# Recurrent stage of a two-block model: order of row loads, key blocks, the first preparation and two clearing steps

## The reference, cut to what matters

```python
mod = cond @ ada_w[l] + ada_b[l]            # shift, scale, gate of a layer, 3072 values
h = rms_norm(x, norm_g[l]) * (1.0 + scale) + shift
z = h @ even_w_in[j]
a_val, a_glu, a_gate, r, k, v, wd, ad, b_gate = split_cols(z, EVEN_SIZES)
ya = conformer_conv(a_val, a_glu, conv_w[j], conv_vec[j]) * silu(a_gate)
...
r, k, v, wd, ad = (lerp(t, mu) for t in (r, k, v, wd, ad))   # z + (shifted z - z) * mu
w_log = -softplus(-(w0 + tanh(wd) @ w_up)) - 0.5
decay = exp(-exp(w_log));  a = sigmoid(a0 + ad @ a_up)
kk = heads(k * k_k);  kk = kk / max(sqrt(sum(kk * kk)), 1e-12)
k = k * (1.0 + (a - 1.0) * k_a)
# scan over 512 tokens, for each of 16 heads of 64:
sa = state @ (-kk);  state = state * w + sa (kk * a)^T + v k^T;  y = state @ r
bonus = sum(r * k * r_k) * v
```

## Time and profile before

| | us |
|---|---|
| median of 3 runs | 3185.33 |
| lowest and highest | 3184.12, 3186.64 |
| the profiled execution | 3184.31 |
| its span in the trace | 3182.5 |
| busy PE in it | 3065.3 (96%) |

### The profile page before, as it was taken

How to read it: one execution, slowest core, us unless ns; L and a number is a source line. 1 busy time by engine, 2 the same in 40 slices (tenths; PEclk the granted TensorE clock), 3 DMA queues, 4 the chain that set the end, 5 groups by cost and what they waited for, 6 DMA issues and landing times.

```text
span 3182.5 us, 38153 instructions
## 1 busy us (share of the span) xinstructions
PE 3065.3 (96%) x15318; PEld 2415.8 (76%) x15318; DVE 2131.8 (67%) x3453; ACT 1236.4 (39%) x1768; POOL 862.2 (27%) x550
## 2 busy tenths in 40 slices
PE   8799999999999999999999999999999999999997
PEld 4467877677677666877887788878888888888886
DVE  3678888758789766574889899456665444444445
ACT  3234444335333655424333566533223222233224
POOL 2243443222344110143455422322222110111100
PEclk9899999999999999999999999999999999999998
DMA  7121111335222111332244467766554334333341
GB/s 258 60 96 53 51 50 58 112 101 173 75 86 73 40 40 35 107 104 90 83 139 133 138 217 231 241 220 198 185 193 152 108 124 126 119 126 119 113 132 53
DMA packets 167568, 382.91 MB, mean 120 GB/s; under 512 B 10848, under 2 KB 77408, under 8 KB 167264
## 3 DMA queue, kind: packets, MB, share of 16 engines
q1 hardware_dynamic: 167392, 380.48, 37.1%
HBM read 320.14 MB, written 60.29 MB: 120 GB/s over the span
## 4 chain that ended last, share of the span: by engine, by line
PE 75%; DVE 15%; ACT 5%; POOL 2%; DMA 2%; issue 1%; SPq 0%; DVEq 0%; ACTq 0%; POOLq 0%
PE ps L747 20%; PE ps L749 20%; PE ps L748 20%; DVE oh L2416 2%; PE ps L1148 2%; DVE at L2154 2%; PE ps L1076 2%; DVE ai L2152 1%; PE ps L915 1%; PE ps L1056 1%; PE ps L935 1%; POOL wsp L2517 1%; PE ps L889 1%; POOL pk L2633 1%; DVE at L2142 1%
## 5 line engine op out<-in xcount | busy, mean ns | idle before, releaser
L747 PE MATMUL ps<-hT,wsp 128*128 128x512 f32 x2016 | 825.7, 410 | 35.8 <-POOL wsp L2517 16.2
L2517 POOL TENSOR_TENSOR wsp<-ring,wsp 128x1024 fp32r<-128x1024 f32 x207 | 512.8, 2480 | 1061.4 <-ACT wsp L1203 1016.7
L749 PE MATMUL ps<-hT,wsp 128*128 128x512 f32 x2016 | 790.8, 392 | 0.0
L748 PE MATMUL ps<-hT,wsp 128*128 128x512 f32 x2016 | 789.5, 392 | 0.0
L747 PEld LDWEIGHTS ps<-hT,wsp 128*128 128x128 f32 x2016 | 381.0, 189 | 142.9 <-issue 24.2
L749 PEld LDWEIGHTS ps<-hT,wsp 128*128 128x128 f32 x2016 | 380.4, 189 | 82.9
L748 PEld LDWEIGHTS ps<-hT,wsp 128*128 128x128 f32 x2016 | 381.6, 189 | 80.5 <-issue 9.1
L2640 POOL TENSOR_TENSOR ex<-ex 128x512 fp32r<-128x512 f32 x128 | 176.0, 1390 | 831.4 <-ACT ex L1600 831.4
L1203 ACT ACTIVATE wsp<-ring 128x1024 fp32r<-128x1024 f32 x311 | 321.8, 1051 | 99.0 <-PE ps L749 80.7
L2440 DVE TENSOR_TENSOR xT<-ps,xT 128x512 f32<-128x512 f32 x256 | 174.7, 688 | 259.8 <-PE ps L749 259.8
L747 PE MATMUL ps<-ex 128*128 128x512 f32 x808 | 314.9, 390 | 2.0 <-DVE ex L1660 2.0
(11 more groups left out here) (406 smaller groups left out, 4784.1 us busy)
## 6 DMA issues: line engine op xcount, KB each, us to landing
ring<-in_eu SPq DMA_DIRECT2D x128, 512.0 KB, 3.6
ring<-in_ev SPq DMA_DIRECT2D x128, 512.0 KB, 3.6
gd<-oh SPq DMA_DIRECT2D x8, 4096.0 KB, 15.0
ex<-gd SPq DMA_DIRECT2D x32, 1024.0 KB, 6.7
ring<-in_ein SPq DMA_DIRECT2D x57, 512.0 KB, 3.7
ring<-in_oin SPq DMA_DIRECT2D x39, 512.0 KB, 3.5
ex<-zd SPq DMA_DIRECT2D x17, 1024.0 KB, 9.3
ring<-in_ada SPq DMA_DIRECT2D x30, 512.0 KB, 3.7
```

Of the source, the lines that this page charges most:

```text
L747: pe.matmul(out, W[0], R[0], start=first, stop=False)
L748: pe.matmul(out, W[0], R[1], start=False, stop=False)
L749: return pe.matmul(out, W[1], R[0], start=False, stop=last)
L2517: pool.tensor_tensor(s[:, 1, :], raw_of(i), s[:, 0, :].bitcast(F32), ALU.subtract).then_inc(pool_done, G.step("lo", i))
```

## The change

Four edits, all in the recurrent stage.

1. **Row loads.** `number` numbers the units in the order of their first use. The four row loads of a group are now put singly before the four quarters of one dense block (`among`): in iteration 1 three groups among the blocks of r, v and `val`, in iteration 7 three among r, v and the gate block, in iteration 8 one among the second gate block. Before, they followed each other with only what `PLACES` put between.
2. **Key first.** The blocks of a pair come as k, r, v in place of r, k, v. The parities of `z_copy` stay as they are.
3. **First preparation.** The blocks k, r and v of pair 0 join the lane of the first preparation, and `PLACES["first"]` spreads its pieces from place 190 to 900 of the whole; before, all but the last stood in the stretch of `val` and `glu` of two blocks behind k, r and v.
4. **Clearing.** `blank` is done for one matrix set at a time: set 0 before `mu`, set 1 at place 900 of the first preparation. The byte mask is a piece of its own (`mask`), behind the v block.

```diff
-    "first": (283, 303, 346, 351, 359, 425, 425, 513, 523, 523, 523, 523, 523, 523, 810, 863, 872, 882),
+    "first": (190, 235, 275, 316, 340, 360, 380, 434, 480, 560, 580, 600, 620, 640, 710, 730, 760, 790, 900),
...
     def number(pieces):
-        loads = []
-        for x in pieces:
-            if x[0] == "ada" or x[0] == "dense" and x[3] == 0:
-                rows = 0
-                while x[0] == "dense" and rows < min(2, len(loads)) and loads[-1 - rows][0] == "ada":
-                    rows += 1
-                loads.insert(len(loads) - rows, x)
-        at = {x: unit("ada" if x[0] == "ada" else "ein", x[4]) for x in loads}
         for x in pieces:
             if x[0] == "ada":
-                order.append((*x[:4], at[x]))
+                order.append((*x[:4], unit("ada", x[4])))
             elif x[0] == "dense":
                 if x[3] == 0:
-                    open_[x[1], x[2]] = at[x]
+                    open_[x[1], x[2]] = unit("ein", x[4])
...
     def rkv(c):
-        return [*dense("r", c, 24 + c), *dense("k", c, 32 + c), *dense("v", c, 40 + c)]
+        return [*dense("k", c, 32 + c), *dense("r", c, 24 + c), *dense("v", c, 40 + c)]
...
+    def among(row, block):
+
+        return [x for pair in zip(row, block) for x in pair]
...
+    order.append(("blank", 0))
     number(dense("mu", 0, 48))
-    number(rkv(0))
-    order.append(("blank",))
-    lane = [*conv_in(0), *conv_in(1)]
-    number([x for _, x in sorted(spread(lane) + placed(prep(0), "first"), key=lambda y: y[0])])
-    mods = {7: [1, 2, 3], 8: [4]}
+    lane = [*dense("k", 0, 32), *dense("r", 0, 24), *dense("v", 0, 40), ("mask",), *conv_in(0), *conv_in(1)]
+    number([x for _, x in sorted(spread(lane) + placed([*prep(0), ("blank", 1)], "first"), key=lambda y: y[0])])
     for i in range(1, 10):
+        rows = {1: [(0, 4), (0, 5), (1, 0)], 7: [(1, 1), (1, 2), (1, 3)], 8: [(1, 4)]}.get(i, [])
...
-        lane = turned_late(lane)
+        lane = turned_late([x for b in range(0, len(lane), 4) for x in (
+            among(ada(*rows[b // 4 - 1]), lane[b:b + 4]) if 0 < b // 4 <= len(rows) else lane[b:b + 4])])
...
-            def blank():
-                for z in abk:
-                    dve.memset(z, 0.0).then_inc(vector_done, V.step())
+            def blank(z):
+                dve.memset(abk[z], 0.0).then_inc(vector_done, V.step())
+                own()
+                for e in range(2):
...
+            def mask():
                 w.wait_ge(tensor_done, T("pp", 7))
                 w.wait_ge(pp_out, 128)
                 w.wait_ge(rw_in, 96)
                 dve.tensor_copy(msk, msum.bitcast(U32)).then_inc(vector_done, V.step("msk"))
...
             def ab(c, d, cc):
-                w.wait_ge(vector_done, V("blank"))
+                w.wait_ge(vector_done, V("blank", c % 2))
+                w.wait_ge(vector_done, V("msk"))
```

More of the change, by code:

```diff
@@ L160, in number @@
     def number(pieces):
-        loads = []
-        for x in pieces:
-            if x[0] == "ada" or x[0] == "dense" and x[3] == 0:
-                rows = 0
-                while x[0] == "dense" and rows < min(2, len(loads)) and loads[-1 - rows][0] == "ada":
-                    rows += 1
-                loads.insert(len(loads) - rows, x)
-        at = {x: unit("ada" if x[0] == "ada" else "ein", x[4]) for x in loads}
+        n = None
         for x in pieces:
             if x[0] == "ada":
-                order.append((*x[:4], at[x]))
+                order.append((*x[:4], unit("ada", x[4])))
             elif x[0] == "dense":
                 if x[3] == 0:
-                    open_[x[1], x[2]] = at[x]
+                    open_[x[1], x[2]] = unit("ein", x[4])
                 order.append((*x[:4], open_[x[1], x[2]]))
@@ L220, in schedule @@
     order.append(("rw_begin",))
+    order.append(("blank", 0))
     number(dense("mu", 0, 48))
-    number(rkv(0))
-    order.append(("blank",))
-    lane = [*conv_in(0), *conv_in(1)]
-    number([x for _, x in sorted(spread(lane) + placed(prep(0), "first"), key=lambda y: y[0])])
-    mods = {7: [1, 2, 3], 8: [4]}
+    lane = [*dense("k", 0, 32), *dense("r", 0, 24), *dense("v", 0, 40), ("mask",), *conv_in(0), *conv_in(1)]
+    number([x for _, x in sorted(spread(lane) + placed([*prep(0), ("blank", 1)], "first"), key=lambda y: y[0])])
     for i in range(1, 10):
+        rows = {1: [(0, 4), (0, 5), (1, 0)], 7: [(1, 1), (1, 2), (1, 3)], 8: [(1, 4)]}.get(i, [])
         lane = [*(rkv(i) if i <= 7 else gates(range(STORED)) if i == 8 else []),
-                *(x for g in mods.get(i, ()) for x in ada(1, g)),
                 *(dense("bgate", i - 2, 47 + i) if 2 <= i < 9 else []), *(conv_in(i + 1) if i <= 6 else [])]
-        if i == 1:
-            lane = [*dense("r", 1, 25), *ada(0, 4), *dense("k", 1, 33), *ada(0, 5), *dense("v", 1, 41), *ada(1, 0), *conv_in(2)]
         if i == 9:
@@ L1791, in rw_begin @@
                 V.here("zero")
-            def blank():
-                for z in abk:
-                    dve.memset(z, 0.0).then_inc(vector_done, V.step())
+            def blank(z):
+                dve.memset(abk[z], 0.0).then_inc(vector_done, V.step())
+                own()
+                for e in range(2):
+                    dve.tensor_copy(mats[z][0][:, e, :, 0, :], ident[:, :].rearrange("p (o n) -> p o n", o=1).broadcast_to(
+                        [128, CH, 128])).then_inc(vector_done, V.step("blank", z))
+            def mask():
                 w.wait_ge(tensor_done, T("pp", 7))
@@ L1799, in blank @@
                 dve.tensor_copy(msk, msum.bitcast(U32)).then_inc(vector_done, V.step("msk"))
[L1800 to L1804, removed]
             def dense_part(kind, i, p, n):
@@ L2491, in vector_program @@
             walk({"ada": ada, "turned": turned, "turned5": turned5, "square": square, "stat": stat, "freed": freed, "raw": raw,
-                  "norm": norm, "norm_nf": norm_nf, "rw_begin": rw_begin, "blank": blank, "dense": dense_part, "tap": tap,
+                  "norm": norm, "norm_nf": norm_nf, "rw_begin": rw_begin, "blank": blank, "mask": mask, "dense": dense_part, "tap": tap,
                   "knr": knr, "mix": mix, "decay": decay, "inv": inv, "hats": hats, "bonus": bonus, "ab": ab, "p1": p1,
```

## The result

| | us |
|---|---|
| before, median of 20 runs | 3184.34 (3178.57 to 3190.19) |
| after, median of 20 runs | 3189.99 (3182.70 to 3195.40) |
| ratio after / before | 1.0018, interval 1.0011 to 1.0025 |
| profiled execution of after, its span | 3188.88, 3187.1 |

The forecast was 3169.3, faster, in a range of 3160 to 3181; the kernel is slower by some 6 us, about the 0.2% that can be told from no change. By the profile's page PE is busy for as large a share as before, and for 5.5 us longer.

A forecast was written before the change was run, and what follows sets the result against it. PE, busy for 96% of the span, bounds the kernel; only its waits and lower clock can be recovered. Gains 2 + 12 + 0 + 2 = 16 us off 3184.3 give 3168.3, plus 1.0 for the median: 3169.3, range 3160 to 3181.

The forecast's parts named there:

- First preparation: Stretch before iteration 1: first `ab` at about 115.0 in place of 117.05, gain 2 us, bounds 7 and a loss of 2.
- The chain: First preparation: scans end at 90.9, `hats` at 98.0, so `bonus` waits about 9.4 us and `turn` 0 another 0.9.
- The clock behind the wait: First preparation, PE work behind the wait at `bonus`: half clock costs about 1.8 us, as behind the 7.35 us.
- Iteration 1: Recurrent stage, iteration 1: 77.9 us in place of 89.79, a gain of 12 us, bounds 15.5 and 6.
- signs of error: Wrong if a low-half wait were 4 us, iteration 1's clock stayed 0.92, or `bonus` came before 94 or after 102 us.
- ideal work: Iteration 1 without PE's idle time and clock loss: 89.8 - 15.2 - 6 = 68.6 us.
- The term of 2 us for the pairs pulled apart: Iteration 1: back-to-back row loads cost less than two apart, so splitting the pairs was taken to cost 2 us.
- Iterations 7 and 8: Recurrent stage, iterations 7 and 8: gain 6.7 + 2.2 - 5.5 - 1.4 = 2 us, bounds -3 and +6.
- the 6.7 us of waits that I struck out: Iterations 7 and 8: all PE idle time, 128.60 - 121.95 = 6.7 us, counted as gain.
- The new halves eat more: Rival: waits of v 1, val 2, v 7 and gate block each bring about 3 us half-clock loss; 3179, chance 0.15.
- Slower: Rival: high halves start only after PE's preceding piece, hiding nothing at five blocks; 3195.6 us, chance 0.06.
- The fill of set 0: Rival: the fill delays POOL's low half of k, PE loses 3.3 us at first k block; 3172.6, chance 0.04.

The follow-up runs named there:

- late_bonus: Changed kernel with `bonus` and the three `turn` moved among the last `glu` block's quarters, second clearing at place 30: 3190.68 us, 1.0022 of before.
- prep_late: Changed kernel with decay, `inv` and `hats` behind `glu` 0, `bonus` and `turn` at 955 to 995, second clearing at 30: 3177.88 us, 0.9976 of before.
- turned_on: Changed kernel with dense units numbered up to two row loads earlier and each `turned` one piece of the lane later: 3174.91 us, 0.9974 of before.
- pulled: Changed kernel with before's `number`: dense units behind row loads loaded and split up to two row loads earlier: 3181.27 us, 0.9989 of before.
- best_a: turned_on with row loads in a row in iterations 7 and 8 and the places of late_bonus: 3172.19 us, 0.9966 of before.
- best_b: turned_on with the places of prep_late and row loads in a row in iteration 7 alone: 3164.91 us, 0.9935 of before.

## Why the prediction was wrong, step by step

**First preparation (forecast a gain of 2, measured 0.1 to 1.7).** The chain was right: `bonus` at 97.56 for 98, a wait of 9.55 for 9.4, `turn` at 0.78 for 0.9, scans at 6.61 for 5 or more. The rule of the Trainium skill, "SBUF — State Buffer", section "Who interferes with whom", that a VectorE instruction with two SBUF inputs contends with a GpSimd instruction that reads SBUF, is borne out once more by 6.61 against 1.45 us. The clock behind the wait was mis-sized: 1.8 us were taken from the wait of 7.35 us, but PE worked at the lower level from 97.6 to about 106.8 (clock 0.51 there), which is some 4 us of loss. In eight profiles the preparation took 64.5 us on the mean, against 65.7 in two of the old order: a gain of about 1. And one move had no price at all: the product of `glu` 0 now stood behind the whole preparation, with val 1 behind it on PE. late_bonus shows that wait, and prep_late against late_bonus that this place was worth 9.4 us.

**Iteration 1 (forecast 77.9, measured 90.7).** The load waits went, `ab` waited 1.91 us for 1.9 forecast, and none stood at v 1 (1.6 forecast). The terms that failed: val 2, 5.47 for 1.7, since I followed ACT's order to the low half and not POOL's, where `mix` stood ahead and waited for DVE; `turned` before `lora`, 1.59 for 0.6; the rest 3.7 for 1.5. Sum of waits 12.7 for 7.3. With 68.6 + 2 of work that makes 83.3, and the remaining 7.4 us are the clock, 0.91 of full, where I had taken the loss of 6 us as gone. Both, a wait of over 4 us on a low half and this clock, were named ahead as signs of error. With the low halves early and `turned` moved the same sum nearly closes: 68.6 + 2 + 8.5 = 79.1, clock 0.98, measured 80.3. So the forecast's ideal work was right to some 2 us; its waits and its clock were not those of this order. The term of 2 us for the pairs pulled apart isn't borne out: from start to next start the twelve row loads took 13.4 us after and 12.8 before, and only one pair of them stood back to back in the trace of before.

**Iterations 2 to 6**: 0, as forecast.

**Iterations 7 and 8 (forecast a gain of 2, measured a loss of 7.6).** Single row loads: from start to next start, the 16 of them took 15.55 us for 14.18 before, 1.4 as forecast. The gate block: 2.38 for 2.4. What failed: of the 6.7 us of waits that I struck out, 1.7 were waits of the inversion (0.78 us and less) that no edit touched, and 2.1 of such waits, with two of the solution, stand in the new trace; v 7 took 2.74 for 1.0, because ACT's square root with its table load stood ahead of the high half; the waits at `turned` and behind it came to 3.2 for 2.1; and the clock, where 2.2 us were to come back, lost 2 more. These are 2.1 + 1.7 + 1.1 + 4 = 8.9 of the 9.6 us missed; the rest isn't assigned.

**Rivals.** "The new halves eat more" named the mechanism, but priced it at 3179 with 0.15: it counted no other term as mis-sized. "Slower" (3195.6) needed 3.6 us exposed at five blocks; the trace has 5.5, 2.7 and 2.4 at three of them and none at v 1 and `glu` 2. The fill of set 0 held nobody up: 3.47 us, beside two low halves of 2.38 us each, the fill as in the kernel before, the halves as on the mean (DVE, then POOL):

```profile
54.33 3.47 DVE L1788 MEMSET rw<- 128x4096 f32 x1 [0.80 <-issue]
57.84 2.87 DVE L1791 COPY rw<-ident 128x512 f32<-128x512 f32 x2
```

```profile
54.48 4.76 POOL L2512 TENSOR_TENSOR wsp<-ring,wsp 128x1024 fp32r<-128x1024 f32 x2 [7.19 <-ACT wsp L1197]
```

**What stays open.** The profiled stages leave after 7.6 us behind before at 730 us, the profiled executions differ by 4.6 and the medians by 5.7: some 2 to 3 us come back in the rest of the kernel, whose order is the same, unexplained. And by what the clock falls: see below.

## What to carry to other kernels

When an edit takes away a wait for a transfer by spreading the transfers, ask at once when each engine *between* transfer and use gets to its step: here ACT's high half and POOL's low half stood in fixed orders behind steps that wait for DVE, and moved with them. A wait is only removed if the next thing in the queue has its bank, its halves and its shared tile; so follow the bank's reader through that engine's own order (prep_late's 12 us) before moving the piece that waits. And strike out only those waits that you can name one by one.

## What the runs showed of the hardware

The lower clock stood behind waits that I had thought too short for it: 1.59 us (0.54 over the 7 us behind), 2.38 (0.56) and 2.74 (0.50). But the length doesn't decide. In the kernel before, a wait of 1.82 us in iteration 7 left it at full (window behind it):

```profile
629.80:638.00 8.20, 8.14 (x53) 7.00 (x54) 5.56 (x9) 1.72 (x4) 3.10 (x2) 1.00 0.28 109
```

In turned_on a wait of 2.57 us left it at full too, and the wait of 1.91 us at `ab` did in after and turned_on, while in pulled the same wait, of the same length, was followed by 0.76 over 7 us. The waits of 0.78 and 1.86 us in iterations 7 and 8 left it at full in turned_on and not in pulled, as told above. best_a and best_b share the order of iteration 1 and took 79.9 and 82.4 us, at 0.98 and 0.94. The scatter between executions of one kernel may come from this, but no run here shows what else decides.

The two copies of the identity of set 0 took 2.87 us beside POOL's second low half and the difference behind it; the same two for set 1, with POOL idle, took 0.76 us, while the fill took 3.47 us beside POOL and without it:

```profile
104.65 0.76 DVE L1791 COPY xT<-ident 128x512 f32<-128x512 f32 x2
```

The Trainium skill, "SBUF — State Buffer", section "Who interferes with whom", has both: an instruction with at most one input from SBUF, outside the two-port modes, doesn't contend with GpSimd, and a copy can enter such a mode. These rows agree.
